# First stage of a hybrid decoder step: order of loads, splits and sums of squares before the first projection tile

## What is computed

```python
def rmsnorm(x, g):
    xf = x.astype(jnp.float32)
    y = xf * lax.rsqrt(jnp.mean(xf * xf, axis=-1, keepdims=True) + RMS_EPS)
    return (y * g.astype(jnp.float32)).astype(x.dtype)

def a_qkv(x, pos, norm_g, w_qkv, qn, kn):
    n, t, _ = x.shape
    qkv = (rmsnorm(x, norm_g) @ w_qkv).reshape(n, t, 3, N_HEADS_A, HEAD_DIM)
    q = rope(rmsnorm(qkv[:, :, 0], qn), pos)
    k = rope(rmsnorm(qkv[:, :, 1], kn), pos)
    return q, k, qkv[:, :, 2]
```

## Time and profile before

| | us |
|---|---|
| three runs, median | 1805.28 |
| three runs, lowest and highest | 1804.64 and 1810.08 |
| the profiled execution, time | 1809.19 |
| the profiled execution, span | 1807.5 |
| first projection matmul (L241) in the trace | 19.19 |

### The profile page before, as it was taken

One profiled execution on the slowest core, in us unless ns is written; L12 is line 12 of the kernel. 1 busy time (PEld: TensorE's weight loads), 2 busy tenths in 40 slices (PEclk: granted clock), 3 DMA queues, 4 the chain that ended last, 5 costly groups with the idle time before them and its releaser, 6 DMA issues.

```text
span 1807.5 us, 24840 instructions
## 1 busy us (share of the span) xinstructions
PE 1710.8 (95%) x9068; PEld 1431.7 (79%) x9068; DVE 1365.8 (76%) x1732; ACT 1038.7 (57%) x1043; POOL 56.0 (3%) x81
## 2 busy tenths in 40 slices
PE   7998989999989798589999999999999999999998
PEld 6876779999987677467887888888878878878886
DVE  5864426565567685688898898898898888888987
ACT  5433324433444242457777777777777767777775
POOL 0001101000000110100000000000000000000000
PEclk9999869999999887699999999999999999999999
DMA  9346413543653421169999999999999999999995
GB/s 326 111 155 189 141 37 126 165 149 114 191 171 117 154 98 44 47 233 330 354 350 331 364 340 343 352 347 331 364 335 344 353 338 351 347 337 354 351 334 205
DMA packets 232982, 452.97 MB, mean 251 GB/s; under 512 B 7585, under 2 KB 79265, under 8 KB 232785
## 3 DMA queue, kind: packets, MB, share of 16 engines
q1 hardware_dynamic: 224656, 421.93, 66.8%
q0 software_dynamic: 8256, 30.12, 5.1%
HBM read 447.30 MB, written 4.72 MB: 250 GB/s over the span
## 4 chain that ended last, share of the span: by engine, by line
PE 86%; DVE 8%; ACT 3%; issue 2%; DMA 1%; POOLq 0%; DVEq 0%; SPq 0%; ACTq 0%; POOL 0%
PE psum L241 24%; PE psum L243 23%; PE psum L242 23%; PE psum L602 2%; PE psum L541 2%; PE psum L740 1%; PE psum L775 1%; PE psum L558 1%; PE psum L755 1%; DVE wlo L237 1%; ACT whi L233 1%; DVE rs L1152 1%; PE psum L583 1%; PE psum L479 1%; PE psum L488 1%
## 5 line engine op out<-in xcount | busy, mean ns | idle before, releaser
L237 DVE TENSOR_TENSOR wlo<-raw,whi 128x2048 fp32r<-128x2048 f32 (+1 forms) x404 | 911.7, 2262 | 208.1 <-ACT whi L233 207.7
L233 ACT ACTIVATE whi<-raw 128x2048 fp32r<-128x2048 f32 (+1 forms) x404 | 764.9, 1896 | 304.4 <-PE psum L243 304.3
L241 PE MATMUL psum<-whi,xgh 128*128 128x512 f32 x896 | 359.7, 401 | 8.5 <-DVE wlo L237 7.1
L243 PE MATMUL psum<-whi,xgl 128*128 128x512 f32 x896 | 355.7, 397 | 0.0
L242 PE MATMUL psum<-wlo,xgh 128*128 128x512 f32 x896 | 354.5, 396 | 0.0
L241 PE MATMUL psum<-hh,whi 128*128 128x288 f32 x800 | 248.4, 310 | 13.7 <-DVE hl L1296 9.1
L243 PE MATMUL psum<-hh,wlo 128*128 128x288 f32 x800 | 241.8, 302 | 0.0
L242 PE MATMUL psum<-hl,whi 128*128 128x288 f32 x800 | 241.1, 301 | 0.0
L241 PEld LDWEIGHTS psum<-whi,xgh 128*128 128x128 f32 x896 | 169.1, 189 | 50.6 <-DVE wlo L237 10.6
L243 PEld LDWEIGHTS psum<-whi,xgl 128*128 128x128 f32 x896 | 168.8, 188 | 41.1
L242 PEld LDWEIGHTS psum<-wlo,xgh 128*128 128x128 f32 x896 | 169.2, 189 | 39.1
(11 more groups left out here) (297 smaller groups left out, 1751.8 us busy)
## 6 DMA issues: line engine op xcount, KB each, us to landing
raw<-in_w_gu_moe SPq DMA_DIRECT2D x226, 1024.0 KB, 5.2
raw<-in_w_down_moe SPq DMA_DIRECT2D x112, 1024.0 KB, 5.3
raw<-in_w_gu_dense SPq DMA_DIRECT2D x22, 1024.0 KB, 5.1
raw<-in_w_qkv_a SPq DMA_DIRECT2D x12, 1024.0 KB, 12.8
raw<-in_w_down_dense SPq DMA_DIRECT2D x16, 704.0 KB, 4.6
kraw_a<-in_cache_a_k POOLq DMA_DIRECT2D x16, 512.0 KB, 4.6
vraw_a<-in_cache_a_v POOLq DMA_DIRECT2D x16, 512.0 KB, 4.8
raw<-in_w_q_b SPq DMA_DIRECT2D x6, 1024.0 KB, 5.0
```

Source lines behind the costliest of these rows:

```text
L233: nc.scalar.activation(whi[:, p % SPL, 0:size], raw[:, p % RAW, 0:size], ACT.Copy).then_inc(hi_ready, 1)
L237: nc.vector.tensor_tensor(wlo[:, p % SPL, 0:size], raw[:, p % RAW, 0:size], whi[:, p % SPL, 0:size].bitcast(F32), ALU.subtract).then_inc(p ...
L241: nc.tensor.matmul(out, lh, rh, start=start, stop=False)
L243: return nc.tensor.matmul(out, ll, rh, start=False, stop=stop)
```

## The change

The constants are put in another order: 13 columns stand first, the eight of the first gain, four head gains and eps, 52 bytes for each partition. The first load brings these alone, then come piece 0, xT, piece 1, the other constants and pieces 2 to 5. ScalarE and VectorE wait for the 13 columns, TensorE at the start for nothing. VectorE sets a small buffer, warm, to 1.0 and ScalarE takes its square root, ahead of all else. Piece 0 is split by both engines before the activations. VectorE alternates gain k and lo half k-1; ScalarE makes all eight hi halves and then the eight squares. TensorE does the sums of squares after tile 0, behind a wait for the other constants; VectorE waits for them before the reciprocal.

```diff
--- before.py
+++ after.py
@@ -60,13 +60,14 @@
 
 CONST = {}
 _at = 0
-for _name, _n in (("ident", P), ("headsum", 32), ("headspread", P), ("featsum", P), ("rot", P), ("cos", T), ("sin", T), ("before", P),
+for _name, _n in (("g_attn_a", KD), ("qn_a", 1), ("kn_a", 1), ("qn_b", 1), ("kn_b", 1), ("eps", 1),
+                  ("ident", P), ("headsum", 32), ("headspread", P), ("featsum", P), ("rot", P), ("cos", T), ("sin", T), ("before", P),
                   ("ones", P), ("slots", P), ("pick", NSAMP), ("expert", NE * 3), ("over", 2 * NE * 2),
-                  ("g_attn_a", KD), ("g_ffn0", KD), ("g_kv", KD), ("g_attn_b", KD), ("g_ffn1", KD),
-                  ("qn_a", 1), ("kn_a", 1), ("qn_b", 1), ("kn_b", 1), ("eps", 1)):
+                  ("g_ffn0", KD), ("g_kv", KD), ("g_attn_b", KD), ("g_ffn1", KD)):
     CONST[_name] = (_at, _at + _n)
     _at += _n
 NCONST = _at
+NFIRST = KD + 5
 MASK_A = 384 + NSAMP * NSEQ
 REGION = 96256
 MASK_B = GB * 384 + PAST + NSAMP * NSEQ
@@ -190,6 +191,7 @@
         tab = at("tab", 96192, [P, 16], I32)
         pgt = sb("pgt", [1, 2 * NSEQ], I32)
         qs = sb("qs", [P, 2])
+        warm = sb("warm", [P, 2])
 
         psum = ctx.enter_context(nc.psum_tensor("psum", [P, 8, 512], F32))
         ps = [psum[:, i, :] for i in range(8)]
@@ -281,9 +283,12 @@
 
         @block.sync
         def _(eng):
-            eng.dma_start(cst[:, :], io["const"]).then_inc(sem("const_loaded"), 16)
+            eng.dma_start(cst[:, 0:NFIRST], io["const"][:, 0:NFIRST]).then_inc(sem("gains_loaded"), 16)
+            load_piece(eng, 0, 0, W[0])
             eng.dma_start(xT[:, :, :], io["xT"]).then_inc(sem("x_loaded"), 16)
-            for p in range(RAW):
+            load_piece(eng, 0, 1, W[1])
+            eng.dma_start(cst[:, NFIRST:NCONST], io["const"][:, NFIRST:NCONST]).then_inc(sem("const_loaded"), 16)
+            for p in range(2, RAW):
                 load_piece(eng, 0, p, W[p])
             eng.dma_start(A["mask"][:, :], io["mask_a"]).then_inc(sem("mask_loaded_a"), 16)
             for p in range(RAW, PRE):
@@ -418,7 +423,6 @@
 
         @block.tensor
         def _(eng):
-            eng.wait_ge(sem("const_loaded"), 16)
 
             def take(n, p):
                 eng.wait_ge(pieces_split, PER * n + p + 1)
@@ -459,6 +463,10 @@
                                         xh[:, k], xl[:, k], k == 0, k == KD - 1)
                         fresh.add(name)
                         ins.then_inc(tile_sem(tiles, m), 1)
+                        if m == 0 and b is A:
+                            eng.wait_ge(sem("const_loaded"), 16)
+                            for k in range(KD):
+                                norm_sum("norm_a", k)
                         if m == 0 and b is B:
                             norm_total("norm_b", 2 * KD - 2)
                     if m % 4 == 0 and 1 <= m // 4 <= nrot // 4:
@@ -648,8 +656,6 @@
                                     k == 0, k == kn - 1)
                     ins.then_inc(tile_sem(tiles, m), 1)
 
-            for k in range(KD):
-                norm_sum("norm_a", k)
             project(A, tiles_a, lambda m: ("norm_a", hh, hl))
             to_tokens(A)
             attend(A, con("ident", A["rows"])[:, 0:A["hq"]])
@@ -839,7 +845,9 @@
 
         @block.scalar
         def _(eng):
-            eng.wait_ge(sem("const_loaded"), 16)
+            eng.wait_ge(sem("q_gains"), 1)
+            nc.scalar.activation(warm[:, 1:2], warm[:, 0:1], ACT.Sqrt)
+            eng.wait_ge(sem("gains_loaded"), 16)
             done = [0]
 
             def split_upto(p):
@@ -971,11 +979,12 @@
                 eng.wait_ge(sem(f"o_copied_{b['tag']}"), b["nj"])
                 nc.scalar.activation(xh[:, 0:b["nj"]], b["oT"][:, :, :], ACT.Copy).then_inc(sem(f"o_hi_{b['tag']}"), 1)
 
-            eng.wait_ge(sem("x_loaded"), 16)
-            eng.wait_ge(sem("q_gains"), 1)
+            split_upto(0)
+            eng.wait_ge(sem("q_gains"), 2)
+            for k in range(KD):
+                norm_hi("norm_a", k, hh)
             for k in range(KD):
                 square("norm_a", k)
-                norm_hi("norm_a", k, hh)
             split_upto(1)
             norm_root("norm_a")
             project(A, lambda r: qs[:, 0:1] if r < 8 else gain("kn_a", 0))
@@ -1094,7 +1103,8 @@
 
         @block.vector
         def _(eng):
-            eng.wait_ge(sem("const_loaded"), 16)
+            nc.vector.memset(warm[:, :], 1.0).then_inc(sem("q_gains"), 1)
+            eng.wait_ge(sem("gains_loaded"), 16)
             done = [0]
 
             def split_upto(p):
@@ -1301,12 +1311,16 @@
 
             V.tensor_scalar(qs[:, 0:1], gain("qn_a", 0), SCALE, None, ALU.mult)
             V.tensor_scalar(qs[:, 1:2], gain("qn_b", 0), SCALE, None, ALU.mult).then_inc(sem("q_gains"), 1)
-            eng.wait_ge(sem("x_loaded"), 16)
-            for k in range(KD):
-                norm_gain("norm_a", "g_attn_a", k)
-            for k in range(KD):
-                norm_lo("norm_a", k, hh, hl)
+            split_upto(0)
+            for k in range(KD + 1):
+                if k == 0:
+                    eng.wait_ge(sem("x_loaded"), 16)
+                if k < KD:
+                    norm_gain("norm_a", "g_attn_a", k)
+                if k >= 1:
+                    norm_lo("norm_a", k - 1, hh, hl)
             split_upto(1)
+            eng.wait_ge(sem("const_loaded"), 16)
             norm_factor("norm_a")
             project(A, tiles_a)
             to_tokens(A)
```

## The result

| | before | after |
|---|---|---|
| median of 22 runs each | 1807.33 | 1810.68 |
| lowest and highest | 1802.3 and 1811.9 | 1805.49 and 1813.88 |
| profiled execution, span | 1807.5 | 1808.2 |
| first projection matmul in the trace | 19.19 | 12.58 |

The ratio is 1.0019, with a 95% interval from 1.001 to 1.0027: in this comparison the changed kernel is slower, by 3.35 us on the medians, 1.8 to 4.9 by the interval. A second comparison further down gives 1.0007 (0.9994 to 1.002). TensorE starts its projection 6.6 us earlier and the kernel ends later.

The account below looks back on a forecast made before the run. The prediction took VectorE and ScalarE's steps in the first stage as the bound: TensorE's 7.1 us earlier start is given back, the ring is 0.3 later, so 1805.28 + 0.3 = 1805.6 us, range 1801.5 to 1809.5.

Parts of the forecast that it names:

- hi of piece 3: Start of piece 3's hi split on ScalarE, where the ring begins: forecast at 28.9 us, against 28.64 before.
- the second load: ScalarE's table load at 18.62 us ahead of the root, 1.28 us long: claimed to disappear with the dummy square root.
- rival 1: First stage: TensorE's earlier start carries through to tile 2, -3.8 us, 1801.5; chance 8%.
- The sum: First stage's net effect: TensorE's 7.1 us earlier start given back to open sums and waiting, ring +0.3, net +0.3 us.
- a late piece: Piece 0 landing at the upper bound of 7.1 us instead of 6.6: net effect +0.8 us.
- a slower turn: Alternating gain, hi and lo before tile 0 taking 0.70 us per turn for 0.64: adds 0.4 us.
- What bounds the kernel now: Opening step on the first 50 us: VectorE's wait for TensorE at tile 1, 1.48 us, is all its slack.
- Those 1.48 us are all the slack: VectorE's wait for TensorE at tile 1: an earlier TensorE is worth no more unless VectorE also norms earlier.
- rival 2: TensorE's clock falls behind its idle 2.6 to 2.8 us after tile 3: +1.3 us on top, 1806.9; chance 22%.
- the ring: VectorE and ScalarE steps with a split on each, until the projection's matmuls take over at 49.08: claimed 0.3 us later.
- The three runs: Earlier runs of the kernel before, 1804.64, 1805.28 and 1810.08 us; the forecast put its sum on their median.
- its dearest rival: Sums of squares behind tile 0 run at the low clock: +3.4 us, 1809.0; chance 5%.

Follow-up runs that it names:

- after_again2: Changed kernel, unchanged, traced again and measured afresh against the kernel before: ratio 1.0007 (0.9994 to 1.002).
- before_again1: Kernel before, unchanged, run again for a second trace of its start: hi of piece 3 at 27.33 us.
- before_fill: Kernel before with four more matmuls, results unread, in TensorE's hole between the sums of squares and tile 0: ratio 0.9986 (0.9971 to 1.0001).
- front_before: Kernel before, cut off behind the first projection with its turning to tokens and key/value stores: median 138.63 us.
- the cut kernels: Kernel before, changed kernel and filled versions, ended behind the first projection and its stores: medians 138.63 us before, 141.50 changed.
- squares_between: Changed kernel with squares alternating with the hi halves again, as in the kernel before: ratio 0.9998 (0.9987 to 1.001) to the kernel before.
- front_after: Changed kernel, cut off behind the first projection with its turning to tokens and key/value stores: median 141.50 us.
- dummy_only: Kernel before with the dummy square root alone: ratio 0.9992 (0.9981 to 1.0004).
- one-sum kernels: Changed kernel with one sum of squares instead of eight, without or with squares alternating with hi halves: hi of piece 3 at 29.47 or 27.19 us.

## Why the prediction was wrong

*What held.* The steps of the changed kernel did, one by one. Piece 0 landed at 6.80 (forecast 6.6), tile 0 began at 12.58 (12.1), the squares ended at 19.1 (18.6), the sums at 21.9 (21.2), L1147 came at 27.33 and 27.69 (26.9 and 27.25), hi of piece 3 at 29.35 (28.9), the chain passed to the projection's matmuls near 49.8 (49.4). VectorE idled 4.01 us (4), TensorE 2.63 us (2.6 to 2.8). The dummy removed the second load. TensorE's lead did not carry (rival 1). The loads behind piece 0 landed later than worked out, without harm here: piece 1 at 13.8 (12.7), the other constants at 17.2 (14.9), piece 2 at 20.3 (18). The constants had 0.7 us to spare before the sums of squares, 0.2 in after_again2.

*The sum's own size.* +0.3 was +0.71: piece 0 landed 0.2 later than I took, and TensorE's start behind that, with the first handovers from gain to hi to lo, another 0.3. That lies within the bounds given (+0.8 with a late piece, +0.4 for a slower turn).

*The step that failed is in "What bounds the kernel now".* "Those 1.48 us are all the slack" was read from one trace as a property of the kernel. It was a property of TensorE's clock in that execution: the same trace shows 0.50 up to 22.6, and I used that stretch to price rival 2 and did not ask what the kernel before would be without it. Its hi of piece 3 would be at 27.3 to 27.5 instead of 28.64, as in before_again1, in before_fill and in front_before. Against that the ring is not 0.3 but 1.65 us late in the cut kernels and 1.8 to 2.0 in the whole ones.

*The chance of rival 2.* What it described came, at +1.1 to +1.2 for the +1.3 worked out; 22% seems to have been too little. It came in one of three traces of the whole changed kernel, in that of squares_between too, and, as far as their times and mean clocks tell, in four of five runs of front_after.

*The starting point.* The three runs had a median of 1805.28, the 22 had 1807.33. Of the 5.08 us between the forecast and the measured time, 2.05 are this and 3.03 the effect (3.35 for 0.3). The text allowed 2 us for a median of three, but ended the range at 1809.5, only 0.5 above its dearest rival. Even 2.05 and rival 2's 1.3 on top of the forecast make 1809.0; the missing step, 1.4 us, would bring that to 1810.4. That all three came together in most of the 22 runs is not shown.

*What stays open.* The first stage explains +0.7 (kernel before low, no fall behind tile 3) to +3.0 us (the reverse: L496 at 50.02 in after_again2, L488 at 47.01 in before_again1). With the shares of the whole-kernel traces, one of four at the full clock and one of three with the fall, it is 0.7 + 0.3 + 0.4 = +1.4; the cut kernels say +2.87. The two whole comparisons say +3.35 (1.8 to 4.9) and +1.3 (-1.1 to +3.6). The two intervals overlap from 1.8 to 3.6 us, and the 2.87 lies there. The 1.4 doesn't, but the traces are too few to say how often each clock occurs in the whole kernel. So the first stage's loss is measured, how it divides in the whole kernel stays open, and a part from behind the first stage isn't excluded. No run points to one: of all traces of the two kernels, the one with the latest first stage (after_again2) has the second shortest span, 1802.9.

## What to carry to other kernels

An engine that starts seven microseconds earlier brings nothing when another engine has the same list of work before the first common step; find that engine, and move work off it. Here that was the table load ahead of the squares and VectorE's and ScalarE's order, not TensorE's start. Before slack is read from a trace, look whether the granted clock was full where it arises, and take a second trace if it was not: a wait for TensorE at half clock isn't slack. A lead that is not used up becomes one long hole, and a hole can have a price of its own. For small effects at the start, cut the kernel off behind the stage and measure that.

## What the runs showed of the hardware

- In the first 50 us of the 18 traces the granted clock fell to 0.50 only behind a hole of TensorE of 1.83 to 3.16 us, and not behind each of them. Before tile 0 it fell behind 2.17, 1.87 and 3.16 us and stayed behind 2.73 (before_again1), 2.89 (dummy_only) and 2.66 (front_before). Behind tile 3 it fell with 2.62 (after_again2) and 2.63 (squares_between) and stayed with 2.63 in three traces. The two one-sum kernels had it too, with 1.98 and 1.83 us ahead of their first L487. The longer hole was not the likelier one. In the five traces with filled holes it stayed full, which alone proves little; in the cut kernels the filling brought the scatter from 1.89 us (140.26 to 142.15) to 0.11 us.
- The granted clock is not the whole pace of TensorE. In the changed kernel the first 18 matmuls of tile 0 start 0.24 us apart, from 12.58 to 16.80, and from 17.25 on 0.13 apart, while every stretch of 1 us from 12 to 18 shows 1.00.
- In layer 0's attention the eight exponentials of the sample part (L942 before, L950 after) stand 14.1 to 14.2 us apart or 15.8 to 16.2, the long kind just twice in each of the 14 traces of whole kernels; only the first one or two distances are anything from 11.5 to 15.1. The last of the eight starts between 238.3 and 242.4 us. So a scatter of 4 us is there by then, a part of that of the whole kernel. The mean granted clock of the 22 runs of the changed kernel goes with their time (correlation -0.85); which causes which is not shown.
- A load of 128 rows of 52 bytes landed 1.8 us after its issue, and the megabyte issued 0.45 us after it landed 5.3 to 5.6 us after its own, in nine traces. The 5.0 that the prediction took is the median of six such loads further on the earlier trace rows.
